# Triangular inversions of four chunks at once in place of two, in a two-layer recurrent decoder on one core

## The chip, the cores and the metric

The kernel runs on one core of one Trainium2 chip. The metric is the device time of one execution in microseconds (us). The core's engines work side by side and meet at semaphores: TensorE (PE; its weight loads are shown as PEld), VectorE (DVE), ScalarE (ACT), GpSimd (POOL) and SyncE (SP), which issues the transfers between HBM and the on-chip memory (SBUF). Matrix products land in PSUM: two tensors here, psA for wide products and psB for small ones, of four banks of 512 columns each.

## The reference

Each of two layers normalizes 512 prompt rows and 8 sample rows of width 1024, projects them, feeds four token mixers, and merges the four results with gates. Two of the mixers, here branch A (RWKV-7) and branch D (gated delta rule), need the inverse of a lower triangular 64 x 64 matrix for each chunk of 64 rows and each of 4 heads. For branch D:

```python
    kb = kc * bc[..., None]
    a_mat = jnp.where(strict, jnp.einsum('nbhid,nbhjd->nbhij', kb, kc) * decay, 0.0)
    m = a_mat + jnp.eye(C, dtype=a_mat.dtype)
    u = lax.linalg.triangular_solve(m, vc * bc[..., None], left_side=True, lower=True)
    w = lax.linalg.triangular_solve(m, kb * jnp.exp(gc)[..., None], left_side=True, lower=True)
...
    def step(S, inp):
        u_i, w_i, qk_i, q_i, k_i, gl_i = inp
        v_new = u_i - jnp.einsum('bhik,bhkv->bhiv', w_i, S)
        o = jnp.einsum('bhik,bhkv->bhiv', q_i, S) + jnp.einsum('bhij,bhjv->bhiv', qk_i, v_new)
        S = S * jnp.exp(gl_i)[..., None, None] + jnp.einsum('bhik,bhiv->bhkv', k_i, v_new)
        return S, o
```

The inversions of different chunks don't depend on each other. The states S run from chunk to chunk, eight chunks in sequence. Branch A's scan is computed in the same chunked form. The 8 sample rows are one decode step each, done on DVE between the chunk work.

## The kernel before

All order is written by hand: each engine has its own program, and named semaphores (`Track`) join them. A layer has four of the phases that matter here in the whole kernel: phase A and phase D of layer 0, then phase A and phase D of layer 1.

**Inversion.** An inversion pass (`j`) treats `GC = 2` chunks, which are 4 pairs of heads (`q`); one phase has `NG = 4` passes. The inverse is built by doubling blocks over `LV = 6` levels. A pass has 11 steps on PE: `pe_start`, then for levels 1 to 5 `pe_y` and `pe_z`. After `pe_y`, ACT copies the product out of PSUM (`act_y`); after `pe_start` and `pe_z`, DVE puts the new blocks in place with two predicated copies (`dve_t`), into T and V, and the next `pe_y` waits for them. The matmuls of `pe_y` and `pe_z` are 32 x 32 tiles, those of `pe_start` and of the chunk work 64 x 64.

**Chunk work.** For each chunk `gram_a` makes the matrices to be inverted and `rows_a` transposes keys and values; then the state runs through `x1_a`, `u_a` and `o_a`. `x1_a(c)` needs the state that DVE wrote after `o_a(c - 1)` (`st_a`), and ACT's copy of that output. These stand behind an inversion step of a later pass. Branch D has the same functions with `_d`.

**Fill.** Behind each step stands `fill_in()`, one slot of wide matmuls (128 x 260, the projection and gate tiles) that need nothing from the chain. A phase has 12 such tiles, each of 12 parts of 4 matmuls, spread evenly over the slots: `SLOTS_A` = 55 slots and `SLOTS_D` = 53. So a slot holds 2 or 3 parts, that is 8 or 12 wide matmuls.

**Transfers.** SP loads the weights of each tile (512 KB) when an earlier tile is done, and in the second half of phase D it also writes out the tanh of each gate tile (260 KB).

## Time and profile before

| what | value |
|---|---|
| median of 3 runs | 1363.7 us (1363.26 to 1364.95) |
| the profiled execution's own time | 1367.13 us |
| its span in the profile | 1365.3 us |
| PE busy | 1318.9 us, 97% of the span |
| DVE busy | 627.7 us, 46% |
| ACT busy | 450.9 us, 33% |
| POOL busy | 375.3 us, 27% |
| mean granted TensorE clock | 0.988 of full speed |

The profile's page gives busy times by engine and groups of instructions; the trace behind it gives each instruction's start. In the rows, "psB<-tg,ws 32*32 32x16 f32 x32" is a group of 32 matmul records that write psB from tg and ws in tiles of 32 x 32, with 16 columns each. One float32 matmul of the program leaves two such records; a wide matmul (psA, 128x260) leaves one. Durations of neighbours on PE overlap, so what a group costs is read from its start to the start of what follows.

### The profile page before, as it was taken

How to read it: one execution, taken by the hardware profiler on the slowest of the kernel's cores; microseconds unless marked ns; L12 is line 12 of the kernel's file. 1: busy time of each engine (PE TensorE's matmuls, PEld its weight loads, DVE VectorE, ACT ScalarE, POOL GpSimd, SP SyncE). 2: the span in 40 equal slices, each digit the busy share in tenths (PEclk: the TensorE clock that was granted, in tenths of full speed). 3: DMA queues.
4: the chain of work that ended last, by engine and by line, in shares of the span. 5: the costliest groups of instructions: out<-in, count | busy, mean ns of one | idle time of the engine just before them, and what ended most of it. 6: DMA issues, size and time to landing. Idle time of an engine off the chain costs nothing.

```text
span 1365.3 us, 40005 instructions
## 1 busy us (share of the span) xinstructions
PE 1318.9 (97%) x18150; PEld 1194.9 (88%) x18150; DVE 627.7 (46%) x1166; ACT 450.9 (33%) x742; POOL 375.3 (27%) x286
## 2 busy tenths in 40 slices
PE   5899999999999999999989999999999999999996
PEld 4899999989899888888779999999988998888896
DVE  4667514318224316756242972242544242467543
ACT  4333422234322236241234253222542222441323
POOL 0344522123222223111323443222332231321122
PEclk9999999999999999999999999999999999999998
DMA  8953231226431263576863333212263223744742
GB/s 314 322 151 84 76 94 49 55 59 131 113 86 49 65 113 105 167 184 194 295 217 89 98 78 87 57 50 65 71 151 105 59 66 62 152 115 104 200 140 94
DMA packets 275933, 162.60 MB, mean 119 GB/s; under 512 B 86102, under 2 KB 244922, under 8 KB 275252
## 3 DMA queue, kind: packets, MB, share of 16 engines
q1 hardware_dynamic: 275220, 159.00, 42.8%
q8 instruction: 143, 2.34, 0.7%
q10 hardware_dynamic: 544, 1.05, 0.2%
q14 instruction: 26, 0.21, 0.1%
HBM read 135.25 MB, written 24.89 MB: 117 GB/s over the span
## 4 chain that ended last, share of the span: by engine, by line
PE 90%; DMA 3%; DVE 3%; ACT 2%; issue 1%; SPq 0%; ACTq 0%; DVEq 0%
PE psA L973 39%; PE psA L981 20%; PE psA L1023 7%; DMA ring<-in_ada_w 2%; PE psB L899 2%; PE psB L915 2%; PE psB L919 1%; PE psB L1126 1%; PE psB L1136 1%; PE psB L320 1%; PE psB L883 1%; PE psB L1364 1%; PE psB L831 1%; PE psB L1089 1%; PE psB L1328 1%
## 5 line engine op out<-in xcount | busy, mean ns | idle before, releaser
L809 POOL TENSOR_TENSOR w_lo<-ring,w_hi 128x512 fp32r<-128x512 f32 x248 | 331.5, 1358 | 835.5 <-ACT w_hi L1668 790.1
L973 PE MATMUL psA<-h_hi,w_hi 128*128 128x260 f32 x1984 | 425.6, 296 | 6.8 <-DVE h_lo L2108 4.9
L973 PE MATMUL psA<-h_lo,w_hi 128*128 128x260 f32 x1984 | 400.9, 284 | 0.0
L973 PEld LDWEIGHTS psA<-h_hi,w_hi 128*128 128x128 f32 x1984 | 305.7, 189 | 28.0 <-issue 15.3
L973 PEld LDWEIGHTS psA<-h_lo,w_hi 128*128 128x128 f32 x1984 | 307.3, 189 | 0.2
L981 PE MATMUL psA<-h_hi,w_lo 128*128 128x260 f32 x1984 | 276.7, 288 | 0.0
L981 PEld LDWEIGHTS psA<-h_hi,w_lo 128*128 128x128 f32 x1984 | 251.7, 189 | 6.9 <-issue 3.0
L1668 ACT CAST w_hi<-ring 128x1024 fp32r<-128x1024 f32 x120 | 123.8, 1032 | 14.6 <-DMA ring<-in_w_in 14.5
L924 ACT COPY ws<-psB 128x128 f32<-128x128 f32 x80 | 21.5, 269 | 187.8 <-PE psB L899 160.0
L1698 ACT ACTIVATE tg<-psA 128x520 f32<-128x520 f32 x48 | 28.9, 603 | 121.0 <-PE psA L981 120.8
L932 DVE COPY_PREDICATED tg<-tmask,psB 128x128 f32<-128x128 uint8 x40 | 14.2, 356 | 101.2 <-PE psB L919 57.6
L932 DVE COPY_PREDICATED ws<-tmask,psB 128x128 f32<-128x128 uint8 x40 | 14.3, 357 | 82.5 <-PE psB L919 44.7
L809 POOL TENSOR_TENSOR rb_lo<-RB,w_hi 128x512 fp32r<-128x512 f32 x16 | 21.6, 1374 | 86.9 <-ACT w_hi L1668 86.9
L809 POOL TENSOR_TENSOR rb_lo<-RB,ra_lo 128x512 fp32r<-128x512 f32 x16 | 21.0, 1339 | 47.5 <-ACT ra_lo L1668 47.5
L1683 ACT COPY RA<-psA 128x520 f32<-128x520 f32 x18 | 10.7, 594 | 62.3 <-PE psA L981 62.2
L2386 DVE SCALAR_TENSOR_TENSOR ws<-RD,parT,ws 128x511 f32<-128x511 f32 (+2 forms) x36 | 30.9, 924 | 0.7 <-ACT ws L1886 0.6
L1023 PE MATMUL psA<-RA,upw 128*128 128x260 f32 x128 | 30.7, 385 | 0.0
L1023 PE MATMUL psA<-RD,upw 128*128 128x260 f32 x128 | 29.9, 384 | 0.8 <-DVE RA L2185 0.8
L1023 PE MATMUL psA<-RB,upw 128*128 128x260 f32 x128 | 29.8, 388 | 0.3 <-DMA upw<-in_w_up 0.2
L2638 DVE SCALAR_TENSOR_TENSOR xT<-psA,modT,xT 128x260 f32<-128x260 f32 x16 | 7.8, 489 | 48.2 <-PE psA L981 36.7
L1023 PE MATMUL psA<-RC,upw 128*128 128x260 f32 x128 | 29.2, 385 | 0.2 <-DMA upw<-in_w_up 0.2
L981 PE MATMUL psA<-merged_hi,rb_lo 128*128 128x260 f32 x224 | 29.1, 282 | 0.0
(511 smaller groups left out, 2000.9 us busy)
## 6 DMA issues: line engine op xcount, KB each, us to landing
ring<-in_w_in SPq DMA_DIRECT2D x122, 512.0 KB, 4.3
scr_tanh<-tg SPq DMA_DIRECT2D x48, 260.0 KB, 4.7
upw<-in_w_up SPq DMA_DIRECT2D x64, 128.0 KB, 3.2
ring<-in_ada_w SPq DMA_DIRECT2D x16, 512.0 KB, 6.4
RB<-in_w_out SPq DMA_DIRECT2D x16, 512.0 KB, 4.2
RA<-scr_tanh SPq DMA_DIRECT2D x30, 260.0 KB, 3.7
ws<-scr_tanh SPq DMA_DIRECT2D x24, 260.0 KB, 3.5
RB<-in_ada_w SPq DMA_DIRECT2D x10, 512.0 KB, 6.2
```

Of the source, the lines that this page charges most:

```text
L320: last = nc.tensor.matmul(out[g:g + 32, 0:256], c32[:, k0 + k, :], piece[:, k, 256 * f:256 * f + 256], start=start, stop=stop)
L809: nc.gpsimd.tensor_tensor(tile_part(RL[s][:, k], (kind, n)), tile_part(RS[s][:, k], (kind, n)), tile_part(HS[L.hslot[q]][:, k], (kind, n)) ...
L899: last = nc.tensor.matmul(meet(z0[pr, cols], lv, 0), At[pr, q, cols], meet(T4[pr, q, cols], lv, 0), start=True, stop=True)
L915: nc.tensor.matmul(meet(z0[pr, cols], lv, 0), V4[pr, q, cols], meet(Y4[pr, q, cols], lv, 0), start=True, stop=True)
L924: nc.scalar.copy(meet(q64(Y), lv, 0), meet(q64(psB[:, 2, 0:256]), lv, 0)).then_inc(*ta.step("y"))
L932: nc.vector.copy_predicated(meet(q64(T), lv, 0), bc(meet(tmask[:, lv, :], lv, 0), 1, 4), meet(q64(psB[:, 2, 0:256]), lv, 0))
L973: nc.tensor.matmul(out(h), HS[L.hslot[q]][:, p, 0:m], cols(part(p), h), start=(p == 0 and part is hi), stop=False)
L981: last = nc.tensor.matmul(out(h), RL[s][:, k, 0:m], cols(hi(k), h), start=False, stop=(k == KT - 1))
L1023: last = nc.tensor.matmul(out(hf), upw[:, idx % UP_RING, i, :], outs[MERGE[idx][0]][:, i, hf * HALF:(hf + 1) * HALF], start=(i == 0), stop ...
L1668: nc.scalar.copy(tile_part(HS[L.hslot[q]], SPLIT[q]), tile_part(RS[s], SPLIT[q])).then_inc(*aw.step("hi"))
L1698: A(half(th_tile(idx)), psA[:, b:b + 2, 0:HALF], ACT.Tanh, scale=0.5).then_inc(*am.step("th"))
L2386: last = STT(out[:, t, sh:SEQ], raw[:, t, 0:SEQ - sh], par(wname, tap * n + t), out[:, t, sh:SEQ], mult, add)
```

## The change

A pass now treats `GQ = 4` chunks, so a phase has two passes (`NQ = 2`) of 11 steps in place of four, and each step has twice the matmuls. The `z` results of the second kind go to psB bank 1 instead of the upper half of bank 2, since bank 2 is now full; the results of `u` and of the state update move from bank 1 to bank 0, and DVE's state update (`st_a`, `st_d`) waits for ACT's copy of the output before it reads bank 0. Of the 24 trips of a phase (`x1`, `u`, `o` of eight chunks) the first 11 stand beside the steps of the second pass and the last 13 behind it, alone with their fill; before, 18 stood beside steps and 6 behind. The slots are recounted: 40 in phase A and 38 in phase D. T has one buffer, which ACT resets at the end of the first pass (`act_t`). V of both passes and the matrices of all chunks are kept at once, so buffers move (some of branch A's to mg5, RB 6 and RB 7). The decode step's pieces on DVE start at the third step of the first pass (before: at the second pass), and their second half stands at the first seven steps of the second pass. The diff, cut:

```diff
-NG = NC // GC
+GQ = 4
+NQ = NC // GQ
...
             def pe_start(pe, tp, At):
-                for q in range(4):
+                for q in range(2 * GQ):
                     for g in range(2):
-                        last = nc.tensor.matmul(psB[sd(g), 2, q * CH:(q + 1) * CH], At[sd(g), q, :], id64[sd(g), :], start=True, stop=True)
+                        last = nc.tensor.matmul(psB[sd(g), 2, q * CH:(q + 1) * CH], At(q)[sd(g)], id64[sd(g), :], start=True, stop=True)
...
-                for q in range(4):
-                    z0, z1 = psB[:, 2, q * CH:(q + 1) * CH], psB[:, 2, 256 + q * CH:256 + (q + 1) * CH]
+                for q in range(2 * GQ):
+                    z0, z1 = psB[:, 2, q * CH:(q + 1) * CH], psB[:, 1, q * CH:(q + 1) * CH]
...
+            def act_t(act, tp, ta, T):
+                act.wait_ge(*tp.at("y", LV - 2))
+                nc.scalar.copy(q64(T), bc(id64, 1, 2 * GQ)).then_inc(*ta.step("ti"))
...
-            SLOTS_A = 5 + 11 * NG + 6
-            SLOTS_D = 3 + 11 * NG + 6
+            STEPS_INV = 2 * LV - 1
+            SLOTS_A = 5 + 2 * STEPS_INV + 13
+            SLOTS_D = 3 + 2 * STEPS_INV + 13
...
+                beside = {0: (gram_a, 4), 1: (gram_a, 5), 2: (rows_a, 0), 3: (rows_a, 1), 4: (gram_a, 6), 5: (rows_a, 2), 6: (gram_a, 7), 7: (rows_a, 3)}
+                late_rows = {7: 4, 9: 5, 10: 6}
+                for j in range(NQ):
+                    At, V = at_a(j), Va[j]
+                    for k in range(STEPS_INV):
...
+                        elif k % 2:
...
+                            pe_y(pe, pa, da, At, Ta, j, (k + 1) // 2)
+                        else:
+                            pe_z(pe, pa, aa, V, Ya, j, k // 2)
+                        if j:
+                            trip_a(k)
+                            if k in late_rows:
+                                rows_a(late_rows[k])
+                        elif k in beside:
+                            work, c = beside[k]
+                            work(c)
+                        fill_in()
+                for n in range(STEPS_INV, 3 * NC):
+                    trip_a(n)
+                    if n == STEPS_INV + 1:
+                        rows_a(7)
                     fill_in()
...
                 def st_a(c):
                     dve.wait_ge(*pa.at("o", c))
-                    did(da, "sum", T_(Ma[:], psB[:, 1, 256:384].rearrange("p (i x) -> p i x", i=2), Ma[:], add), c)
+                    dve.wait_ge(*aa.at("o", c))
+                    did(da, "sum", T_(Ma[:], psB[:, 0, 384:512].rearrange("p (i x) -> p i x", i=2), Ma[:], add), c)
```

What stands in a row on PE. Phase A of layer 0, around the step `pe_y` of level 3 in the first pass, before (line 899 is `pe_y`, lines 915 and 919 `pe_z`, line 1126 `gram_a`, lines 973 and 981 the wide matmuls):

```order
413 L1126 MATMUL psB<-ws 64x128 x8
414 L981 MATMUL psA<-h_hi,w_lo 128x260 x4
415 L973 MATMUL psA<-h_hi,w_hi 128x260 x2
416 L973 MATMUL psA<-h_lo,w_hi 128x260 x2
417 L973 MATMUL psA<-h_hi,w_hi 128x260 x2
418 L973 MATMUL psA<-h_lo,w_hi 128x260 x2
419 L899 MATMUL psB<-tg,ws 32x2x8 x16
420 L973 MATMUL psA<-h_hi,w_hi 128x260 x2
421 L973 MATMUL psA<-h_lo,w_hi 128x260 x2
422 L973 MATMUL psA<-h_hi,w_hi 128x260 x2
423 L973 MATMUL psA<-h_lo,w_hi 128x260 x2
424 L915 MATMUL psB<-ws,tg 32x2x8 x4
```

The same step of the changed kernel (its lines: 906 is `pe_y`, 922 and 926 `pe_z`, 1141 `gram_a`, 1151 `rows_a`, 990 and 998 the wide matmuls):

```order
453 L1141 MATMUL psB<-ws 64x128 x8
454 L998 MATMUL psA<-h_hi,w_lo 128x260 x16
455 L906 MATMUL psB<-tg,mg 32x2x8 x16
456 L906 MATMUL psB<-tg,ws 32x2x8 x16
457 L1151 MATMUL psB<-cst,ws 64x64 x8
458 L1151 MATMUL psB<-cst,RA 64x64 x4
459 L990 MATMUL psA<-h_hi,w_hi 128x260 x2
460 L990 MATMUL psA<-h_lo,w_hi 128x260 x2
461 L990 MATMUL psA<-h_hi,w_hi 128x260 x2
462 L990 MATMUL psA<-h_lo,w_hi 128x260 x2
463 L990 MATMUL psA<-h_hi,w_hi 128x260 x2
464 L990 MATMUL psA<-h_lo,w_hi 128x260 x2
```

One step has 32 matmuls in place of 16, and the wide runs on its two sides have 16 and 12 in place of 12 and 8.

On DVE, at the end of phase A of layer 0, before (lines 932 and 933 are `dve_t`, 2316 `u_a`, 2320 and 2321 `st_a`):

```order
223 L2316 COPY ws<-psB 128x128
224 L2320 TENSOR_TENSOR M<-psB,M 128x128
225 L2321 TENSOR_TENSOR M<-M,pc 128x128
226 L932 COPY_PREDICATED tg<-tmask,psB 128x8x16
227 L933 COPY_PREDICATED tg<-tmask,psB 128x8x16
228 L933 COPY_PREDICATED tg<-tmask,psB 128x4x32
229 L2316 COPY ws<-psB 128x128
230 L2320 TENSOR_TENSOR M<-psB,M 128x128
231 L2321 TENSOR_TENSOR M<-M,pc 128x128
```

The changed kernel at the same end (942 and 948 are `dve_t`, 2247 `u_a`, 2252 and 2253 `st_a`):

```order
196 L948 COPY_PREDICATED RB<-tmask,psB 128x8x32
197 L2247 COPY ws<-psB 128x128
198 L2252 TENSOR_TENSOR M<-psB,M 128x128
199 L2253 TENSOR_TENSOR M<-M,pc 128x128
200 L2247 COPY ws<-psB 128x128
201 L2252 TENSOR_TENSOR M<-psB,M 128x128
202 L2253 TENSOR_TENSOR M<-M,pc 128x128
203 L2247 COPY ws<-psB 128x128
204 L2252 TENSOR_TENSOR M<-psB,M 128x128
205 L2253 TENSOR_TENSOR M<-M,pc 128x128
```

The predicated copies are over four chunks earlier, and the states of the last five chunks follow each other with nothing between but their own waits.

## Rows read from the trace of the kernel before

**Rows 1.** The page: busy time, share and instructions of each engine.

```profile
PE 1318.9 (97%) x18150; PEld 1194.9 (88%) x18150; DVE 627.7 (46%) x1166; ACT 450.9 (33%) x742; POOL 375.3 (27%) x286
```

**Rows 2.** Windows, the four phases: length, busy by engine, granted clock, DMA share, GB/s.

```profile
166.70:300.88 134.18, 134.18 (x3137) 122.13 (x3137) 38.09 (x102) 33.97 (x77) 31.17 (x24) 1.00 0.24 62
383.54:508.60 125.06, 123.05 (x2813) 111.83 (x2813) 37.50 (x99) 30.27 (x69) 29.41 (x23) 0.99 0.34 78
832.61:966.97 134.36, 134.36 (x3137) 122.24 (x3137) 38.06 (x102) 34.07 (x77) 31.17 (x24) 1.00 0.24 62
1049.00:1175.13 126.13, 124.23 (x2820) 112.59 (x2819) 37.48 (x99) 30.27 (x69) 30.06 (x24) 0.99 0.35 79
```

**Rows 3.** Timeline of PE, phase A, layer 0: y, wide, z, wide, y.

```profile
180.08 0.44 PE L899 MATMUL psB<-tg,ws 32*32 32x16 f32 x32
180.45 0.50 PE L973 MATMUL psA<-h_hi,w_hi 128*128 128x260 f32 x2
...
182.08 0.25 PE L915 MATMUL psB<-ws,tg 32*32 32x16 f32 x8
...
182.74 0.50 PE L973 MATMUL psA<-h_hi,w_hi 128*128 128x260 f32 x2
...
183.89 0.44 PE L899 MATMUL psB<-tg,ws 32*32 32x16 f32 x32
184.26 1.70 PE L981 MATMUL psA<-h_hi,w_lo 128*128 128x260 f32 x12
```

**Rows 4.** Timeline of PE: the last z step of a pass.

```profile
200.53 0.44 PE L910 MATMUL psB<-tg,ws 32*32 32x32 f32 x16
200.90 0.39 PE L973 MATMUL psA<-h_hi,w_hi 128*128 128x260 f32 x1
```

**Rows 5.** Timeline of PE: 16 and 32 records of 64 x 64 before a wide run.

```profile
261.41 0.68 PE L883 MATMUL psB<-cst,ws 64*64 64x64 f32 x16
262.02 0.39 PE L973 MATMUL psA<-h_hi,w_hi 128*128 128x260 f32 x1
...
407.04 1.15 PE L1364 MATMUL psB<-cst,ws 64*64 64x64 f32 x32
408.12 0.51 PE L973 MATMUL psA<-h_hi,w_hi 128*128 128x260 f32 x2
```

**Rows 6.** Timeline of DVE: the two copies of `dve_t` at level 1.

```profile
182.87 0.45 DVE L932 COPY_PREDICATED tg<-tmask,psB 128x128 f32<-128x128 uint8 x1 [3.07 <-PE psB L919]
183.12 0.50 DVE L933 COPY_PREDICATED tg<-tmask,psB 128x128 f32<-128x128 uint8 x1
```

**Rows 7.** Timelines of PE, ACT and DVE between `o_a` and the next `x1_a`.

```profile
292.62 0.50 PE L973 MATMUL psA<-h_hi,w_hi 128*128 128x260 f32 x2
...
294.25 0.33 PE L1152 MATMUL psB<-M,ws 64*64 64x64 f32 x4
...
292.74 0.27 ACT L1832 COPY RA<-psB 128x128 f32<-128x128 f32 x1 [0.26 <-PE psB L1183]
...
292.74 0.29 DVE L2320 TENSOR_TENSOR M<-psB,M 128x128 f32<-128x128 f32 x1 [2.65 <-PE psB L1183]
293.07 0.92 DVE L2321 TENSOR_TENSOR M<-M,pc 128x128 f32<-128x128 f32 x1
```

**Rows 8.** The page's row of PE's instruction queue: packets, MB, share.

```profile
q8 instruction: 143, 2.34, 0.7%
```

**Rows 9.** A stop of PE in phase D, and windows behind it and over one block.

```profile
484.98 0.24 PE L919 MATMUL psB<-ws 32*32 32x16 f32 x6 [1.27 <-issue]
...
485.50:490.50 5.00, 5.00 (x78) 4.63 (x75) 0.75 (x4) 0.80 (x3) 0.00 (x0) 0.66 0.54 59
...
1141.00:1145.50 4.50, 4.50 (x71) 4.12 (x71) 0.47 (x2) 0.80 (x3) 0.00 (x0) 0.62 0.01 4
...
398.75:399.00 0.25, 0.25 (x27) 0.22 (x30) 0.00 (x0) 0.00 (x0) 0.00 (x0) 1.00 0.23 66
```

**Rows 10.** Timeline of SP: the last of the vector transfers for branch D's decode step.

```profile
391.73 0.43 SPq L590 DMA_DIRECT2D vv<-scr_b  x1
```

More of the change, by code:

```diff
@@ L893, in pe_y @@
                             first, second = quarter(g, 0), quarter(g, 1)
-                            last = nc.tensor.matmul(z0[second, lower], At[first, q, upper], T4[first, q, lower], start=True, stop=True)
+                            last = nc.tensor.matmul(z0[second, lower], At(q)[first, upper], T4[first, q, lower], start=True, stop=True)
                         continue
@@ L1244, in _, with trip_a @@
-                for c in (NC - 2, NC - 1):
-                    x1_a(c)
-                    fill_in()
-                    u_a(c)
-                    fill_in()
-                    o_a(c)
+                def trip_a(n):
+                    (x1_a, u_a, o_a)[n % 3](n // 3)
+                for c in range(GQ):
+                    gram_a(c)
+                    fill_in()
+                fill_in()
+                beside = {0: (gram_a, 4), 1: (gram_a, 5), 2: (rows_a, 0), 3: (rows_a, 1), 4: (gram_a, 6), 5: (rows_a, 2), 6: (gram_a, 7), 7: (rows_a, 3)}
@@ L1462, in _ @@
+                for n in range(STEPS_INV, 3 * NC):
+                    trip_d(n)
+                    if n == STEPS_INV + 1:
+                        rows_d(3)
                     fill_in()
@@ L1875, in _, with trip_a @@
-                for c in (NC - 2, NC - 1):
-                    x1_a(c)
-                    after_fill()
-                    after_fill()
-                    o_a(c)
+                tree_start(Ta, Va, aa)
+                for c in range(GQ + 1):
+                    after_fill()
+                rows_at = {2: 0, 3: 1, 5: 2, 7: 3}
+                late_rows = {7: 4, 9: 5, 10: 6}
+                def trip_a(n):
+                    if n % 3 != 1:
+                        (x1_a, None, o_a)[n % 3](n // 3)
@@ new lines, in _ @@
+                for j in range(NQ):
+                    for k in range(STEPS_INV):
+                        if k % 2:
+                            act_y(act, pa, aa, Ya, j, (k + 1) // 2)
+                        if j == 0 and k == STEPS_INV - 2:
+                            act_t(act, pa, aa, Ta)
+                        if j:
+                            trip_a(k)
+                        here = (late_rows if j else rows_at)
+                        if k in here:
+                            rows_a(here[k])
+                        after_fill()
@@ L1880, in _ @@
+                for n in range(STEPS_INV, 3 * NC):
+                    trip_a(n)
+                    if n == STEPS_INV + 1:
+                        rows_a(7)
                     after_fill()
@@ L2365, in _ @@
+                for n in range(STEPS_INV, 3 * NC):
+                    trip_a(n)
                 pd, ad, dd = TR["pe_d"], TR["act_d"], TR["dve_d"]
@@ new lines, in _, with trip_d @@
+                gram_d(1)
+                def trip_d(n):
+                    if n % 3 != 1:
+                        (x1_d, None, st_d)[n % 3](n // 3)
+                beside = {0: (gram_d, 2), 2: (gram_d, 3), 4: (rows_d, 0), 6: (rows_d, 1)}
+                for j in range(NQ):
+                    dve.wait_ge(*ad.at("ti", j))
+                    for k in range(STEPS_INV):
+                        if k % 2 == 0:
+                            dve_t(dve, pd, dd, GRd, 2, Td, Vd[j], j, k // 2)
+                        if j:
+                            trip_d(k)
+                            if k == 7:
+                                rows_d(2)
+                        elif k in beside:
+                            work, c = beside[k]
+                            work(c)
+                        if j == 0 and 2 <= k < 9 or j and k < 7:
+                            decode_d(k if j else k - 2, j)
@@ L2535, in _ @@
+                for n in range(STEPS_INV, 3 * NC):
+                    trip_d(n)
+                    if n == STEPS_INV + 1:
+                        rows_d(3)
                 ac, dc = TR["act_c"], TR["dve_c"]
-                for c in (NC - 2, NC - 1):
-                    x1_d(c)
-                    st_d(c)
                 dve.wait_ge(*ac.at("cv0"))
```

452 lines of the change are left out of this document (135 added, 317 removed).

## The prediction

> **What bounds the kernel now.** I read the page's busy times first: PE is busy for 1318.9 of 1365.3 us and DVE for less than half of that [rows 1]. So only what shortens PE's own row of work, or a wait on it, can move the time. Then I cut out the four phases that the change touches, by windows. The two phases A last 134.18 and 134.36 us, and PE is busy in every microsecond of them: no semaphore costs anything there, neither of DVE's copies nor of ACT's. The two phases D last some 125.6 us each, and PE stands still for 2.01 and 1.90 us in them [rows 2]. The reader is to see that the latency of the inversion is already hidden by the fill. A change that only hides it better has nothing to win in phase A.
>
> So the question is what a step costs PE beyond its matmuls. I read that from starts in the timeline. A run of 12 wide matmuls takes from 180.45 to 182.08, 1.63 us; a run of 8 from 182.74 to 183.89, 1.15 us [rows 3]. Four matmuls make the difference of 0.48, so one costs 0.12, and a run of 8 would be 0.96 without its 0.19. That 0.19 us is lost once per run, whenever PE comes from small tiles to wide ones and goes back. In the same way a y step with 32 records takes 180.45 - 180.08 = 0.37 us and a z step with 64 takes 182.74 - 182.08 = 0.66 us [rows 3]: 0.29 for 32 records, and 0.08 once per step. The last z step, 16 records in tiles with twice the columns and half as many side by side, takes 0.37 as well [rows 4], as if it were 32. For 64 x 64 tiles, 16 records take 0.61 us and 32 take 1.08 [rows 5]: 0.47 for 16 records, and 0.14 once.
>
> As a test of this reading I sum phase A from it. Wide: 576 x 0.12 + 54 runs x 0.19 = 79.4. The 20 y steps are 7.4 and the 20 z steps 16 x 0.66 + 4 x 0.37 = 12.0. The rest (starts, grams, rows, chunk trips) are the other 35 us of the 134.2 [rows 2], and the change leaves their number as it is, save the starts.
>
> **The change, part by part.**
>
> *Matmuls.* Two passes with eight q stand for four with four: no matmul is added or removed. The fill is the same 144 parts.
>
> *Fewer runs.* The slots go from 55 to 40 in phase A and from 53 to 38 in phase D; in each kernel two of them are neighbours, so the wide runs go from 54 to 39 and from 52 to 37. 15 runs x 0.19 = 2.85 us per phase.
>
> *Fewer steps.* 40 y and z steps become 20, each with twice the records: 20 x 0.08 = 1.6 us per phase (y then takes 0.66, z 0.66 + 64 x 0.009 = 1.24). Four starts become two: 2 x 0.14 = 0.28.
>
> *Chunk work.* Its instructions are the same; more of it stands alone between wide runs, but these runs are counted above. Nothing is taken for it.
>
> The sum is 4.73 us per phase, x 4 = 18.9 us.
>
> *Longer copies on DVE.* The two copies of a low level take 0.45 and 0.50 us, the second 0.25 behind the first, and end 0.88 us after the z step (182.74 to 183.62) [rows 6]. With twice the elements I bound each at twice its duration, so the pair ends at most 0.13 + 0.50 + 1.00 = 1.63 us after the step. The cover is a fill of 12 or 16 wide matmuls, 1.63 us or 2.11, and at the low levels chunk work of 8 to 40 records ahead of it. If that chunk work were gone, the low levels would just be even. I take zero; the upper bound is 0.2 x 2 steps x 8 passes = 3.2 us.
>
> *The added wait.* Between `o_a` and the next `x1_a` DVE now waits for ACT's copy. Before, `o_a` ends at 292.62; ACT copies for 0.27 from 292.74 and at the same time DVE starts a sum and a product that end at 293.99, and the next `x1_a` starts at 294.25, behind 12 wide matmuls [rows 7]. With ACT first, everything on DVE comes some 0.4 us later: 294.4, that is 0.15 late behind 12 wide matmuls and in time behind 16. The 0.92 of the product is its long form. Beside a step of the inversion 0.66 us or more is added to the cover; behind the second pass there are four such places in a phase. Queued behind DVE's wait is only the next `u` copy, and PE is the one that waits for that. 4 x 4 x 0.15 = 2.4 us is the bound if every one is the long form with the short fill; I take 0.8, a third. The bound below is nothing.
>
> *Inputs that are wanted earlier.* Branch D's decode begins two steps into the first pass. The last vector transfer is issued at 391.73 [rows 10]. In the new order two grams, three slots, and three steps with two grams stand between 383.5 and that piece, about 2.0 + 5.1 + 8.7 us, so it is wanted near 399; 7 us are enough. Zero.
>
> *PE's instructions.* PE's instruction queue moves 2.34 MB in 143 packets [rows 8]: 16.4 KB each. With one load and one matmul for each of 18150 records [rows 1] this is 64 bytes an instruction and 127 records a block. In quiet time such a block shows as a lone quarter microsecond at 66 GB/s [rows 9]. In phase D PE stops in the middle of a z step, with nothing to wait for, for 1.27 us up to 484.98 [rows 9]. There are six such stops, three in each phase D, which make up the 2.0 and 1.9 us of [rows 2]. After the longest in each, the granted clock is 0.66 for 5 us and 0.62 for 4.5 us [rows 9], 1.7 us lost each time. I read them as instruction blocks that come late behind SP's tile loads; together they cost 3.9 + 3.4 = 7.3 us. They stand in the half of phase D in which tanh tiles are written out too. After the change most of that half is behind the second pass, where a slot has only 8 to 40 small records, so blocks are wanted seldom; this speaks for a gain of up to 7.3. But inside the passes a z step is 128 records, a whole block in 1.24 us, where before the densest stretch (z, 12 wide, y: 108 records) took 0.66 + 1.63 + 0.37 = 2.66 us. This speaks for new stops, in phases A too. I take zero between the two.
>
> The Trainium skill ("Runtime: NRT & Kernel Launch", Instruction fetch mechanics) says that PE's instruction memory holds 128 KiB, filled in blocks of 16 KiB. The block size agrees with [rows 8]; eight blocks ahead would be over 30 us of work and no stop could come, in either kernel. The same section also speaks of only two lines, which fits the stops in [rows 9] better. By the deep memory the sum stays as it is, since the stops would have another cause.
>
> **The sum.** The profiled execution took 1367.1 us: 1367.1 - 18.9 + 0.8 = 1349.0. The median is 3.4 us below the profiled execution, so 1363.7 - 18.1 = **1345.6 us**.
>
> **The rivals.**
>
> *Late instruction blocks eat the gain.* For it: six stops already, and records up to 2.5 times as dense inside the passes (9.7 ns each for 24.6). Against it: phases A have the same loads and not one stop. One late block with its slow stretch is 1.3 + 1.7 = 3.0 us. Three more than now give 1354.6, and that is the likely form. It decides from seven more on: 21 us, 1366.6, slower than before. Each phase has 22 of its 40 or 38 slots inside the passes and so about seven of its 12 tile loads, 28 in all, so seven are possible.
>
> *Late blocks go away.* The stops of phase D vanish because the tanh tiles fall behind the second pass: 1345.6 - 7.3 = 1338.3.
>
> *Waits take the place of the hidden ones.* All bounds of the longer copies and of the added wait at once: 3.2 + 2.4 - 0.8 = 4.8 more; and as much again, 4.8, if ACT is still busy with a tile's evacuation when `o_a` ends. 1345.6 + 9.6 = 1355.
>
> *The change doesn't do what it says.* If the 0.19 and 0.08 were not paid per run and per step but overlapped with something that stays, the kernel would end at 1363 to 1364. Against it: the same two numbers rebuild the 134.2 us of phase A.
>
> **How the numbers follow.** The forecast, 1340 to 1351: 0.70. Some late blocks, 1351 to 1361: 0.11; many, over 1366: 0.04. Blocks that go away, 1336 to 1340: 0.07. Waits, 1351 to 1358: 0.05. Nothing saved: 0.03. The range 1337 to 1355 holds the forecast and most of its two neighbours, 0.83. 0.2% is 2.7 us, about what a measurement of this kernel tells from no change: faster 0.93, same 0.03, slower 0.04.
>
> **What the next profile would show.** Right: phases A near 129.5 us with PE busy throughout; y steps of 0.66 and full z steps of 1.24; wide runs of 12 and 16 at 1.63 and 2.11. The added wait: idle time before `x1_a` or `x1_d` behind the second pass. The blocks: stops "issue" inside z steps, with a granted clock near 0.6 behind them. I am wrong if a step with twice the records takes twice as long, if PE idles in phase A, or if the stops in the two phases D together change by more than 4 us.

## The result, and the profile after

The changed kernel is slower: 1376.5 us median of 11 runs (1368.57 to 1382.66) against 1363.8 of 11 runs of the kernel before (1359.48 to 1366.14) on the same chip. The ratio is 1.0083, with a 95% interval of 1.0057 to 1.0108. The forecast was 1345.6. The profiled execution of the changed kernel took 1382.66 us, the slowest of the 11 and 6 more than their median, so its profile shows more of the harm than a usual execution has. The kernel's executions scatter by 6 to 8 us to either side of their median, those of before by 2 to 4.

The page gives PE's busy time and its instruction queue. They answer to [rows 1] and [rows 8]:

```profile
PE 1313.4 (95%) x18150; PEld 1197.9 (87%) x18150; DVE 620.4 (45%) x1086; ACT 442.9 (32%) x686; POOL 373.9 (27%) x286
q8 instruction: 143, 2.34, 0.7%
```

PE has the same 18150 records, its instruction queue moves the same 143 packets (called blocks from here on), and PE is busy for 5.5 us less, but the span is 15.5 us longer. So PE stands still for some 21 us more than before. The windows of the four phases answer to [rows 2] (length, busy by engine, granted clock, DMA share, GB/s):

```profile
168.16:305.76 137.60, 132.01 (x3138) 122.33 (x3138) 37.40 (x82) 32.15 (x63) 31.74 (x24) 0.98 0.23 60
386.92:514.23 127.31, 120.91 (x2818) 111.94 (x2817) 33.41 (x79) 28.26 (x55) 28.82 (x23) 0.97 0.32 75
838.61:977.16 138.55, 132.58 (x3137) 122.84 (x3137) 37.52 (x82) 32.16 (x63) 31.73 (x24) 0.98 0.23 60
1061.34:1189.33 127.99, 121.80 (x2818) 112.87 (x2818) 34.25 (x79) 28.46 (x55) 28.34 (x23) 0.96 0.32 75
```

The four lengths add up to 531.5 us, against 519.7 in [rows 2]. Length less busy time gives the idle time: 5.59, 6.40, 5.97 and 6.19, together 24.2 us, where [rows 2] has 3.9. And the clock, which was full in phases A, is below 1.00 in every phase. What PE waited for is in its list of waits (line waited at, releaser, us in total, times, longest):

```profile
PE psB L906 <- issue: 8.3, 5, 2.6
...
PE psB L926 <- issue: 8.0, 8, 1.6
...
PE psB L922 <- issue: 3.4, 4, 1.7
...
PE psB L1191 <- issue: 1.5, 1, 1.5
PE psB L1195 <- issue: 1.3, 1, 1.3
...
PE psB L901 <- issue: 0.5, 1, 0.5
```

That is 20 stops of 23.0 us in which PE waited for nothing that the profile shows, 18 of them inside the y and z steps (lines 901, 906, 922, 926). Before, the same list has five stops of 3.8 us, all in phases D. A stretch of the timeline of PE, phase A of layer 0, shows one of them, and what comes behind it:

```profile
185.20 0.44 PE L906 MATMUL psB<-tg,mg 32*32 32x16 f32 x32
185.48 0.45 PE L906 MATMUL psB<-tg,ws 32*32 32x16 f32 x32
185.86 1.09 PE L1141 MATMUL psB<-ws 64*64 64x128 f32 x16
186.88 1.71 PE L998 MATMUL psA<-h_hi,w_lo 128*128 128x260 f32 x12
...
188.99 0.25 PE L922 MATMUL psB<-RB,tg 32*32 32x16 f32 x8
...
190.18 0.68 PE L1151 MATMUL psB<-cst,ws 64*64 64x64 f32 x16
...
192.67 0.36 PE L906 MATMUL psB<-tg,mg 32*32 32x16 f32 x20
195.55 0.34 PE L906 MATMUL psB<-tg,mg 32*32 32x16 f32 x11 [2.52 <-issue]
...
196.31 1.12 PE L1151 MATMUL psB<-cst,ws 64*64 64x64 f32 x16
```

Up to 192.67 all is about as forecast: y takes 0.66 us (185.20 to 185.86), z 1.19 (188.99 to 190.18; the forecast was 1.24), 16 wide matmuls 2.11 (186.88 to 188.99). Then PE stops after 20 of the 64 records of a y step and goes on 2.52 us later. What follows is slow: the same 16 records of L1151 that took 0.52 us at 190.18 take 0.90 at 196.31. Two windows, behind this stop and over one y-to-y pair, show why:

```profile
195.55:201.50 5.95, 5.95 (x84) 5.60 (x83) 0.00 (x0) 0.85 (x2) 0.00 (x0) 0.50 0.01 3
...
185.20:192.67 7.47, 7.47 (x262) 6.90 (x261) 3.08 (x6) 2.40 (x4) 2.43 (x2) 1.00 0.34 96
```

Behind the stop the granted clock is 0.50 for six microseconds, the 1.2 GHz level of the two. The last row is the rate at which a pass wants instructions: 262 records in 7.47 us, or 128 in 3.65 us. The window over the same kind of stretch in the kernel before, y, wide, z, wide of [rows 3]:

```profile
180.08:183.89 3.81, 3.81 (x117) 3.48 (x117) 0.75 (x2) 0.95 (x2) 2.53 (x2) 1.00 0.62 190
```

That is 128 records in 4.17 us, and PE never stops in it.

How a block arrives is seen in a stretch of the changed kernel in which no other transfer runs: windows over the end of a z step and the stop behind it, and the timeline of PE where it goes on.

```profile
232.25:232.50 0.25, 0.25 (x32) 0.22 (x22) 0.00 (x0) 0.00 (x0) 0.25 (x1) 1.00 0.00 0
232.50:232.75 0.25, 0.25 (x11) 0.25 (x12) 0.13 (x1) 0.00 (x0) 0.25 (x1) 1.00 0.22 66
232.75:234.90 2.15, 0.89 (x31) 0.81 (x26) 1.17 (x2) 0.00 (x0) 0.06 (x1) 1.00 0.00 0
...
236.00:236.25 0.25, 0.25 (x4) 0.25 (x3) 0.22 (x2) 0.00 (x0) 0.00 (x0) 1.00 0.22 66
```

```profile
234.97 0.27 PE L1195 MATMUL psB<-ws 64*64 64x64 f32 x2 [1.33 <-issue]
```

The block begins to move between 232.50 and 232.75, and PE goes on at 234.97, some 2.3 us later, with no other transfer in between. A window counts a transfer's bytes and time where it begins, so the block did not move in a quarter microsecond, as [rows 9] were read: 0.22 of 16 engines for 0.25 us is 0.88 us of one engine, and 0.7% of 16 engines' span for 143 blocks is some 1.1 us each. The next block begins to move at 236.00, 1.0 us after PE went on. I read this as a cycle: 1.0 us from entering a block until the next begins to move, 0.9 for the transfer, 1.4 until its first matmul, together some 3.4 us for 128 records.

The long stop at 195.55 is of another kind. SP had issued a tile load and a tanh write when PE entered a block at about 189.5 (128 records before the stop), and the next block began to move only when they were through:

```profile
188.62 0.38 SPq L634 DMA_DIRECT2D ring<-in_w_in  x1
189.25 0.37 SPq L659 DMA_DIRECT2D scr_tanh<-mg  x1
...
189.50:193.25 3.75, 3.53 (x146) 3.20 (x135) 2.90 (x5) 1.14 (x2) 3.01 (x2) 1.00 0.73 211
193.25:193.50 0.25, 0.00 (x0) 0.00 (x0) 0.25 (x1) 0.00 (x0) 0.04 (x1) 1.00 0.25 66
193.50:195.50 2.00, 0.00 (x0) 0.00 (x0) 0.33 (x1) 0.00 (x0) 0.00 (x0) 0.87 0.00 0
```

From entering to the start of the transfer are 3.8 us in place of 1.0; from there to PE's restart are 2.3, as in the quiet stop. The 128 records took 3.56 us, so with a transfer after 1.0 us this stop would hardly have been there. I read the packets of the instruction queue at all 20 stops in the same way, counting back 128 records to where PE entered the block ahead (127 where it had gone on from another stop there), which is good to some tenths of a microsecond. Each ends 2.3 to 2.8 us after its block begins to move. At nine of them, 15.3 of the 23.0 us, other transfers of 460 to 790 KB stood between entering and the block, which began to move 1.7 to 3.8 us after entering. At the other eleven, 7.7 us, nothing over 5 KB did, and it was 0.8 to 1.8 us. In the kernel before, all five stops are of the loaded kind (1.8 to 4.1 us). This is the one of [rows 9]:

```profile
478.20 0.37 SPq L632 DMA_DIRECT2D ring<-in_w_in  x1
478.84 0.36 SPq L657 DMA_DIRECT2D scr_tanh<-tg  x1
...
478.50:482.50 4.00, 3.92 (x99) 3.56 (x88) 0.79 (x3) 1.52 (x3) 2.52 (x2) 1.00 0.77 196
482.50:482.75 0.25, 0.25 (x5) 0.25 (x4) 0.00 (x0) 0.00 (x0) 0.00 (x0) 1.00 0.54 119
```

**Where the time went.** In the profiled executions the phases became 11.7 us longer, in two parts. Idle time grew by 24.2 - 3.9 = 20.3. Busy time fell only by 8.5 (507.3 after, 515.8 in [rows 2]), because part of it ran at half clock. Read in windows of 0.25 us, the clock is down in six stretches (four of 3.4 us, one of 6.8 and one of 10.2) and costs 15.4 us, against two stretches of 3.4 and 3.4 us lost before: 12.0 more. So the work itself shrank by 8.5 + 12.0 = 20.5 us, where the prediction has 18.9. 20.3 + 12.0 - 20.5 = 11.8, and some 3.8 more fell outside the four phases, where nothing was changed.

### The profile page after: what moved, and what is told of

It reads as the page before. It is cut to its first block, busy times and chain, and to the rows that moved or that the text cites. A ratio compares the mean times of both kernels' runs of the same rounds, so it can differ in the third digit from the quotient of the medians.

```text
span 1380.8 us, 39829 instructions
## 1 busy us (share of the span) xinstructions
PE 1313.4 (95%) x18150; PEld 1197.9 (87%) x18150; DVE 620.4 (45%) x1086; ACT 442.9 (32%) x686; POOL 373.9 (27%) x286
## 3 DMA queue, kind: packets, MB, share of 16 engines
q8 instruction: 143, 2.34, 0.7%
## 4 chain that ended last, share of the span: by engine, by line
PE 87%; DMA 4%; issue 2%; DVE 2%; ACT 2%; SPq 2%; ACTq 0%; DVEq 0%
PE psA L990 38%; PE psA L998 19%; PE psA L1040 7%; DMA ring<-in_ada_w 2%; PE psB L906 2%; PE psB L922 2%; PE psB L926 1%; PE psB L1141 1%; PE psB L322 1%; PE psB L1151 1%; DMA RB<-in_ada_w 1%; SPq L407 1%; ACT w_hi L1632 1%; PE psB L890 1%; DMA upw<-in_w_up 1%
## 5 line engine op out<-in xcount | busy, mean ns | idle before, releaser
L990 PE MATMUL psA<-h_lo,w_hi 128*128 128x260 f32 x1984 | 406.4, 287 | 0.0
L990 PEld LDWEIGHTS psA<-h_hi,w_hi 128*128 128x128 f32 x1984 | 312.0, 192 | 25.8 <-issue 15.3
L990 PEld LDWEIGHTS psA<-h_lo,w_hi 128*128 128x128 f32 x1984 | 313.2, 192 | 0.2
L998 PE MATMUL psA<-h_hi,w_lo 128*128 128x260 f32 x1984 | 272.5, 287 | 0.0
L942 DVE COPY_PREDICATED tg<-tmask,psB 128x256 f32<-128x256 uint8 x20 | 11.1, 553 | 79.0 <-PE psB L926 46.3
L942 DVE COPY_PREDICATED ws<-tmask,psB 128x256 f32<-128x256 uint8 x20 | 11.0, 552 | 75.3 <-PE psB L926 60.7
L931 ACT COPY ws<-psB 128x256 f32<-128x256 f32 x20 | 7.5, 376 | 79.5 <-PE psB L906 60.5
L2411 DVE SCALAR_TENSOR_TENSOR M<-M,kdl,psB 128x64 f32<-128x64 f32 x32 | 7.6, 278 | 56.7 <-ACT RD L1874 56.7
L2301 DVE SCALAR_TENSOR_TENSOR ws<-RD,parT,ws 128x511 f32<-128x511 f32 (+2 forms) x36 | 30.9, 925 | 0.7 <-ACT ws L1832 0.6
```

Source lines behind the costliest of these rows:

```text
L942: nc.vector.copy_predicated(meet(q64(T), lv, 0), bc(meet(tmask[:, lv, :], lv, 0), 1, 2 * GQ), meet(q64(psB[:, 2, :]), lv, 0))
L990: nc.tensor.matmul(out(h), HS[L.hslot[q]][:, p, 0:m], cols(part(p), h), start=(p == 0 and part is hi), stop=False)
L998: last = nc.tensor.matmul(out(h), RL[s][:, k, 0:m], cols(hi(k), h), start=False, stop=(k == KT - 1))
L2301: last = STT(out[:, t, sh:SEQ], raw[:, t, 0:SEQ - sh], par(wname, tap * n + t), out[:, t, sh:SEQ], mult, add)
```

## The experiments

Theory T (S in the texts that were written ahead of the runs): a block of some 127 instruction records can only be had every so often. Inside the longer passes PE uses them up faster than that, and behind some of the stops the clock is down too. Rival L: blocks are late because SP's tile loads are ahead of them, as the prediction read it. The two don't exclude each other: a load can lengthen the time that a block takes, and the density decides whether PE notices. Rival B: the moved results (psB bank 0) and DVE's added wait do the damage. All ratios are to the kernel before, run on the same chip in the same job.

**burst: the supply by itself.** The kernel before, with 512 additional matmuls (1024 records) that nothing reads, behind phase A of layer 0, where the DMA engines are nearly idle:

```diff
                 last.then_inc(*pa.step("mt"))
+                if layer == 0:
+                    for n in range(512):
+                        g, e = n % 2, n // 2 % 2
+                        pr = quarter(g, e)
+                        nc.tensor.matmul(psB[pr, 2, 16 * (n // 4 % 16):16 * (n // 4 % 16) + 16], id64[pr, lower], id64[pr, 0:16], start=True, stop=True)
```

> The kernel before, with 512 extra small matmuls (1024 records, 8 instruction blocks of 127 records; 32 x 32 tiles, 16 columns, four tiles in turn, constant operands, results never read) on TensorE behind phase A of layer 0, where no tile load runs. It measures how fast instructions can be supplied. Theory S (supply: in the changed kernel's stops a block becomes usable about 3.6 us after the one ahead of it is entered, load or no load): after one or two blocks the burst goes at one block in 3.6 us, so it lasts 22 to 29 us and shows stops of 2 to 2.5 us that end 2.4 us behind each lone block transfer. Theory L (blocks only come late behind tile loads): nothing delays them here, 1024 x 0.009 = 9.5 us without a stop.

1393.7 us in one run, 30 more than the kernel before. The timeline of PE over the additional records, and a window over all of them:

```profile
300.94 1.34 PE L1260 MATMUL psB<-cst 32*32 32x16 f32 x139
303.86 1.25 PE L1260 MATMUL psB<-cst 32*32 32x16 f32 x128 [1.57 <-issue]
307.58 1.90 PE L1260 MATMUL psB<-cst 32*32 32x16 f32 x128 [2.48 <-issue]
311.04 1.90 PE L1260 MATMUL psB<-cst 32*32 32x16 f32 x128 [1.56 <-issue]
...
321.95 1.90 PE L1260 MATMUL psB<-cst 32*32 32x16 f32 x128 [1.83 <-issue]
325.40 1.78 PE L1260 MATMUL psB<-cst 32*32 32x16 f32 x117 [1.55 <-issue]
```

```profile
300.94:327.12 26.18, 13.81 (x1026) 13.04 (x1025) 0.00 (x0) 5.37 (x9) 2.49 (x2) 0.58 0.10 24
```

This is the row to remember: PE runs exactly 128 records, stops, and runs the next 128. From one restart to the next it takes 3.45 to 3.73 us, whether the 128 records take 1.25 us (full clock) or 1.90 (half). By the queue's packets that is 1.0 to 1.1 us until the next block begins to move, 0.9 to 1.3 for the transfer and 1.3 to 1.5 until its first matmul. The additional 1024 records take 26.2 us instead of some 10. The changed passes want 128 records in 3.65 us, which is inside that range. The first stop comes after 139 records, so no more was in hand than the rest of one block and one more.

Of this the Trainium skill ("Runtime: NRT & Kernel Launch", Instruction fetch mechanics) says that blocks are of 16 KiB and that crossing into a new one is mostly hidden. The block's size agrees with this case (143 blocks are 2.34 MB). That it is hidden holds for most crossings of the kernel before, and for none of the seven here from the 139th record on.

**bank0: the moved results alone.** The kernel before, with u and the state's sum in psB bank 0 and the added wait, nothing else:

```diff
                     dve.wait_ge(*pa.at("o", c))
-                    did(da, "sum", T_(Ma[:], psB[:, 1, 256:384].rearrange("p (i x) -> p i x", i=2), Ma[:], add), c)
+                    dve.wait_ge(*aa.at("o", c))
+                    did(da, "sum", T_(Ma[:], psB[:, 0, 384:512].rearrange("p (i x) -> p i x", i=2), Ma[:], add), c)
```

> The kernel before with one part of the change alone: the results of u and of the state update lie in psB bank 0, and the state update on VectorE waits for ScalarE's copy of the output. Passes of two chunks as before. Theory S: within 2 us of the kernel before, 1362 to 1367, because the density of matmul records is as it was; at most some short waits before x1. Rival B (the shared bank or the added wait causes the stops of TensorE): 1370 or more, with stops in phases A.

1365.6 us, ratio 1.0013 (0.9993 to 1.0034). The profile has six small stops (0.2 to 0.7 us), five in phases D, at the lines of those of before, and one of 0.2 in a phase A. B falls: it could explain 5 us at most, not 31.

**light: the changed kernel with easier tile loads.** The loads of the tiles of the phases read their 512 KB as one contiguous piece per partition from another weight, so these tiles are computed from wrong weights.

```diff
+                    if (kind, n) in IN_A + IN_D:
+                        sp.dma_start(RS[s].rearrange("p k c -> p (k c)"), a["w_out"][layer, 0:P, :]).then_inc(arrived, 16)
+                        return
                     sp.dma_start(RS[s], src.rearrange("(k p) c -> p k c", p=P)).then_inc(arrived, 16)
```

> The changed kernel with the tile loads made lighter inside phases A and D: each of the 24 tiles of a layer that fill these phases is loaded as 128 rows of 4 KB from another weight (so the projections of these tiles are computed from the wrong weights), where before it was 1024 rows of 512 bytes. Same bytes, in an eighth of the descriptors, so each load keeps the queues busy for a shorter time. Theory S: most stops stay, since they come with the queues quiet as well: 1370 to 1380. Theory L: the stops go with the load, and the kernel falls to 1345 to 1355.

1367.3 us, ratio 1.002 (0.9997 to 1.0043): some 9 us less than the changed kernel, a little below what T expected and far above what L alone did. The profile has 17 stops of 15.0 us, where the changed kernel has 20 of 23.0; but this profile is of the fastest of ten executions (1361.8 us) and that one of the slowest of 11, so the difference of the two flatters the edit. One stop in the same place as the one at 195.55:

```profile
193.26 0.27 PE L909 MATMUL psB<-tg,mg 32*32 32x16 f32 x11 [1.56 <-issue]
```

It took 1.56 us in place of 2.52 (its twin in layer 1: 1.59 in place of 2.60), and the clock behind it stayed at 1.00. The nine loaded stops of the changed kernel are all there again and all but one shorter, 9.1 us in place of 15.3: their blocks began to move 1.4 to 2.9 us after entering, in place of 1.7 to 3.8. The quiet ones make up 5.9 us, where the changed kernel has 7.7. So loads make a block later, and where they do they lengthen the stop. The loads still moved as many bytes, so this is not a test without load; the quiet stop at 234.97 and burst are.

**coarse: fewer records, more work.** The changed kernel with the y and z steps of levels 1 to 4 in 64 x 64 tiles, half as many records in these steps, each longer:

```diff
-                    for e, cols in enumerate((lower, upper)):
-                        for g in range(2):
-                            pr = quarter(g, e)
-                            last = nc.tensor.matmul(meet(z0[pr, cols], lv, 0), At(q)[pr, cols], meet(T4[pr, q, cols], lv, 0), start=True, stop=True)
+                    for g in range(2):
+                        pr = sd(g)
+                        last = nc.tensor.matmul(meet(z0[pr], lv, 0), At(q)[pr], meet(T4[pr, q], lv, 0), start=True, stop=True)
```

> The changed kernel with the y and z steps of levels 1 to 4 in tiles of 64 x 64 in place of 32 x 32: half the instructions for the same products (the blocks off the diagonal that this adds are masked away by the copies). Two tiles side by side in place of four, so a y step should take 0.9 to 1.1 us for 0.66 and a z step 1.8 to 2.0 for 1.2, which adds 20 to 39 us over four phases. Semaphores, passes, banks and fill stay as in the changed kernel. Theory S: the records in a pair of slots fall from about 250 to 150, and the stops inside the steps vanish: TensorE idle under 1 us in each phase A, where the changed kernel has 5.6. Rival B (banks, waits or the length of the passes cause the stops): the idle time stays near 5 us a phase.

1371.7 us in one run. Its list of waits has no "issue" at all, its clock is full in all four windows (those of layer 0):

```profile
167.66:304.30 136.64, 136.19 (x2370) 127.44 (x2369) 38.10 (x82) 32.33 (x63) 30.87 (x24) 1.00 0.23 60
388.47:512.92 124.45, 124.45 (x2049) 116.68 (x2049) 33.25 (x79) 28.25 (x55) 28.78 (x23) 1.00 0.32 76
```

A y step takes 0.95 us with 32 records, a z step about 1.9 with 64, so PE does 0.29 and 0.7 us more per step, 8 x 0.99 = 7.9 per phase, 31.7 in all. The prediction's own sum then closes: 1363.6 - 18.9 - 7.3 (no stops, no slow clock) + 0.8 + 31.7 = 1369.9. This was decisive for the density: the same passes, the same banks, the same loads, a quarter fewer records in a phase (2370 for 3138), and every stop is gone, the loaded ones too. The sum also agrees with the saving of 18.9 us, within the scatter of a single run.

**weighted: denser fill inside the passes.** The changed kernel with 4 or 5 parts of fill behind each step of a pass and 2 or 4 in the tail, in place of 3 or 4 everywhere:

```diff
-            fill_a, fill_d = Fill(IN_A, SLOTS_A), Fill(IN_D, SLOTS_D)
+            fill_a, fill_d = Fill(IN_A, [2] * 5 + [5 - k % 2 for k in range(STEPS_INV)] * 2 + [4 if n % 3 == 2 and n < 23 else 2 for n in range(STEPS_INV, 24)]), Fill(IN_D, [3, 3, 4] + [5 - k % 2 for k in range(STEPS_INV)] * 2 + [4 if n % 3 == 2 and n < 23 else 2 for n in range(STEPS_INV, 24)])
```

> The changed kernel with only the fill weighted (4 and 5 parts a slot inside the passes, 2 behind most of the work around them); all tiles 32 x 32 as in the changed kernel. Theory S: a full z step is still a block in 1.2 us, less than the 3.6 a block needs, but the long runs behind it let the supply catch up, so the stops get fewer or shorter, not rare: 1358 to 1372. Rival: if the mean density inside the passes alone decided (252 records in 7.9 us, 4.0 us a block), no stop would be left: 1338 to 1350.

1361.1 us, ratio 0.999 (0.9972 to 1.0007), 15 us less than the changed kernel with the same matmuls in another order. Two windows, phases A and D of layer 0:

```profile
167.12:299.23 132.11, 129.56 (x3137) 119.82 (x3137) 40.26 (x82) 32.38 (x63) 30.35 (x24) 1.00 0.24 63
383.29:510.38 127.09, 120.75 (x2818) 111.85 (x2818) 37.37 (x79) 28.51 (x55) 28.40 (x23) 0.97 0.34 77
```

In phase A PE is busy for 129.56 us, the forecast's 129.5, at full clock; the y-to-y pair has 269 records in 8.41 us, 128 in 4.00. Phase D still loses 6.3 us to idle time and some to the clock. The profile has 16 stops of 12.8 us in all, though the mean density is below what burst could be supplied with: a z step is still a block's worth of records in 1.2 us, and at eleven of the 16 stops a load of over 300 KB stood ahead of the block.

**zsplit: half of the slot inside the z step.** As weighted, with half of the slot's fill between the two halves of a z step:

```diff
                 for q in range(2 * GQ):
+                    if q == GQ and lv < LV - 1:
+                        between()
```

> The weighted kernel with each z step of levels 1 to 4 cut in two halves of 64 records and half of the slot's fill between them. This adds 16 wide runs and 16 step beginnings a phase, 16 x 0.27 x 4 = 17 us if all were paid at once (8 z steps a phase are cut: 8 x 0.27 x 4 = 8.6 us). Theory S: 127 records from the start of a z step take about 2.5 us in place of 1.2 to 1.9, so the stops are shorter than in the weighted kernel: 1352 to 1366.

1362.5 us, ratio 0.9993 (0.9978 to 1.0009): no better than weighted. The profile has six stops of 5.7 us in place of 16 of 12.8, so the size of one burst does matter, beside the average over a pair. What was won on the stops was paid back in the steps: the additional change from small tiles to wide ones and back is 0.19 + 0.08 = 0.27 us by the prediction's prices, 2.2 us for the eight split steps of a phase; the phase A of layer 1 is busy for 131.7 us in place of 129.4.

**mix and mix_even: half of each z step coarse.** z of the first four q in 64 x 64 tiles, on weighted's fill (mix) and on the changed kernel's own even fill (mix_even):

```diff
+                    if q < GQ:
+                        for g in range(2):
+                            pr = sd(g)
+                            nc.tensor.matmul(meet(z0[pr], lv, 0), V4[pr, q], meet(Y4[pr, q], lv, 0), start=True, stop=True)
+                        for g in range(2):
+                            pr = sd(g)
+                            nc.tensor.matmul(meet(z1[pr], lv, 1), Y4[pr, q], meet(V4[pr, q], lv, 1), start=True, stop=True)
+                        continue
```

> A version meant to keep the gain without the stops. The changed kernel, with the z steps of levels 1 to 4 for the first four q in 64 x 64 tiles and for the other four in 32 x 32 (96 records in place of 128), and the fill weighted: 4 parts behind each y step and 5 behind each start and z step, 2 behind most of the work ahead of and behind the passes. Theory S: a z step takes about 1.55 us (half of 1.9 and half of 1.2), 0.35 more, 11 us in all; in no stretch do 127 records take much less than 3.6 us, so few stops are left. 1363.6 - 18.9 - 7.3 (the stops of the kernel before) + 11.2 + 0.8 = 1349.4 without a stop, 1349 to 1358 with some. Rival L (stops come with the tile loads, whatever the density): 1370 or more.

> The same half-coarse z steps in the changed kernel with its even fill (3 or 4 parts a slot). It tells what the weighting of the fill is worth. Theory S: 127 records from the start of a z step then take about 3.9 us in quiet time, so stops come only where a tile load delays a block: 1352 to 1362, a few us above the weighted one.

mix took 1359.5 us, ratio 0.9975 (0.9957 to 0.9992); mix_even 1363.9, ratio 1.0009 (0.9993 to 1.0026). They are 1.5 and 1.9 us above the ranges that T expected. Issue stops fell to 1.4 us in mix; in mix_even 4.7 us remained, all in phases A, while its phases D had none and were the shortest (120.66 and 120.39 us).

**both: each phase with what suited it.** Weighted fill and fine tiles in phases A; the even fill and half-coarse z steps in phases D.

```diff
-                            pe_z(pe, pd, ad, V, Yd, j, k // 2)
+                            pe_z(pe, pd, ad, V, Yd, j, k // 2, GQ)
```

> The best parts of the runs so far, by phase. Phase A as in the weighted kernel (32 x 32 tiles, 4 and 5 parts of fill a slot inside the passes), phase D as in the kernel with half-coarse z steps and even fill. In their profiles the phases A of the one lasted 132.1 and 131.8 us, the phases D of the other 120.7 and 120.4; the kernel before has 134.2, 125.6, 134.4 and 125.5. Theory S, if the phases add up: 14.7 us less than before, 1348 to 1352. If the place of the block boundaries in the program moves the stops about (each changed phase shifts all blocks behind it), part of that is lost: up to 1358.

1357.6 us, ratio 0.996 (0.9943 to 0.9977), faster than both kernels; from mix, which ran on another chip, the intervals don't tell it apart. It is 4.9 us less than before, where the sum of the phases had promised 14.7. Its windows:

```profile
169.23:301.93 132.70, 129.63 (x3137) 119.89 (x3136) 40.21 (x82) 32.34 (x63) 30.33 (x24) 1.00 0.24 63
384.49:505.85 121.36, 120.49 (x2561) 112.07 (x2561) 33.41 (x79) 28.26 (x55) 28.79 (x23) 1.00 0.33 78
829.11:962.91 133.80, 131.29 (x3138) 121.41 (x3137) 40.24 (x82) 32.34 (x63) 30.34 (x24) 0.99 0.24 62
1045.46:1165.87 120.41, 120.38 (x2561) 112.02 (x2561) 33.50 (x79) 28.36 (x55) 28.80 (x23) 1.00 0.34 79
```

The four add up to 508.3 us, 11.4 less than [rows 2]; 6.5 are still idle time. Its profile has six stops of 4.6 us, five of them in phases A. Why the medians show less than the phases isn't settled; the profiled execution of before was 3.4 us above its median, which is half of that gap.

**before_light: the light loads in the kernel before.** The edit of light, made in the kernel before (so these tiles are computed from wrong weights too).

> The kernel before with the lighter tile loads inside phases A and D (128 rows of 4 KB from another weight for 1024 rows of 512 bytes, so these tiles are computed from the wrong weights). Theory: its six stops need both a tile load that delays a block and a dense stretch. With the lighter loads the stops in phase D should shrink or go: 1356 to 1361. If they had another cause, the time stays within 2 us of the kernel before.

1361.9 us, ratio 0.9994 (0.998 to 1.0009). Its profile has stops of only 2.3 us, the longest 1.0, and no slow clock in phases D, where the kernel before has 3.9 and 3.4 us. Its median doesn't show these 5 us and is what the other branch expected (within 2 us of before). All four of its stops have a load ahead of their block, lighter as it is. What other executions of the kernel before lose to stops, one profile doesn't tell; this stays unclear.

**thin: the kernel before, with less fill inside its passes.** The old passes of two chunks, 2 parts behind every step, the rest ahead of and behind them:

```diff
+            fill_a, fill_d = Fill(IN_A, [5] * 5 + [2] * (11 * NG) + [5, 5, 5, 5, 5, 6]), Fill(IN_D, [7, 6, 6] + [2] * (11 * NG) + [6, 6, 6, 6, 6, 7])
```

> The kernel before, passes of two chunks, with the fill moved out of the passes: 2 parts in each of their 44 slots (before: 2 or 3) and the rest ahead of and behind them. Number of matmuls, steps and wide runs stay. Theory S (the density of the records makes the stops, not the passes of four chunks): z, 8 wide, y and x1 are 127 records in about 3.1 us, less than 3.6, so stops of up to 0.5 us appear in phases A, which had none; 2 to 8 us in all phases together more than before: 1366 to 1375, besides waits for VectorE or ScalarE, which the profile names as such. Rival (only the change's passes bring stops): phase A stays without a stop that has no releaser.

1366.5 us in one run. Here T expected more stops than came: 1.4 us in the profile's list, none over 0.5, and no slow clock in phase A or D of layer 0. (One more wait of 1.2 us, put down to a copy of ACT at line 924 that was done 0.8 us earlier, ends 2.4 us after a block began to move, as the stops do.) One window shows the density:

```profile
198.76:202.92 4.16, 4.16 (x137) 3.77 (x137) 0.49 (x2) 0.75 (x2) 1.95 (x2) 1.00 0.26 76
```

137 records in 4.16 us are 128 in 3.89. That is denser than before (4.17) but still slower than the supply (3.45 to 3.73). Phase A of layer 0 had stops here that it had not before (0.3, 0.4 and 0.2 us), so density alone brings some, but little. The mean density can't be the whole reason: weighted lost 12.8 us at 128 in 4.00. Its z steps of 128 records, where thin has 64, are what differs by design; that this is the cause isn't shown beyond zsplit.

## Why the prediction was wrong

- **Matmuls, Fewer runs, Fewer steps** (18.9 us): right. The steps took 0.66 and 1.19 us (forecast 0.66 and 1.24), the wide run of 16 took 2.11 as forecast. Phase A, where its blocks keep up, is busy for 129.56 us (forecast 129.5). In the changed kernel itself the saving measures 20.5 us.
- **Longer copies on DVE** (0, bound 3.2): right. No wait of PE in the four phases is put down to DVE's predicated copies.
- **The added wait** (0.8): right, with luck in the exact number, since 0.8 was a third of a bound. PE's waits there are two of 0.8 us in sum for DVE (L1167, `x1_a`). A third of 0.2 (L1383, `o_d`) is for ACT's copy of `u`, which PE waited for in the kernel before as well. The tail of phase A on ACT and DVE shows the order that was foreseen, the sum behind the copy:

```profile
270.56 0.27 ACT L1797 COPY RA<-psB 128x128 f32<-128x128 f32 x1 [0.26 <-PE psB L1197]
...
270.92 0.29 DVE L2252 TENSOR_TENSOR M<-psB,M 128x128 f32<-128x128 f32 x1 [4.19 <-ACT RA L1797]
271.25 0.56 DVE L2253 TENSOR_TENSOR M<-M,pc 128x128 f32<-128x128 f32 x1
```

- **Inputs that are wanted earlier** (0): right, no such wait.
- **PE's instructions** (taken at zero): this is the step that failed. Measured against the kernel before it is 20.3 us of idle time, 1.0 of it the two waits above, and 12.0 of half clock: 31 us in the profiled execution. Between the medians it is 1376.5 - 1345.6 = 30.9; that the two agree is partly luck, since the profile is of the slowest execution.

Why it failed can be named. The prediction read the stops of [rows 9] rightly as instruction blocks that come late behind SP's transfers: all five (it counted six, three in each phase D; the list has two and three) have 410 to 800 KB ahead of their block. What it lacked is that a block takes its time with no load at all, 3.45 to 3.73 us in burst. It supposed that a stop needs a load ahead of its block; eleven of the 20 stops in the changed kernel had none. And it took "phases A have the same loads and not one stop" as a sign that their loads were harmless. They were so only at the old density. With 128 records in 4.17 us at the densest, phases A went through their loads without a stop; at 3.65 the same kind of load costs 2.52 and 2.60 us there. The change went to 3.65 for the very reason for which it was to win: fewer slots of fill inside the passes. Zero "between the two" had no sum behind it.

The demand was set against the wrong measure too. "Up to 2.5 times as dense" compares one z step of the changed kernel (9.7 ns a record) with z, 12 wide and y of the kernel before (24.6). A z step of before takes 0.66 us for 64 records, which is about as dense (10.3 ns); over a pair of steps the rise is from 4.17 to 3.65 us, a seventh.

The rival **Late instruction blocks eat the gain** is what happened; it was said to decide "from seven more on", and there were 15 more. Its price of 3.0 us per stop with its slow clock was somewhat high (31 us for 15 are 2.1 each). Its chance of 0.04 was the mistake.

What the rows of before could have told: the records of a y-to-y pair over its length, next to the places where a load makes a block late. [rows 2] has the other hint: stops come in phases D alone.

What stays open. How the idle time divides between density and loads was read from one execution, the slowest; about two thirds of it stood behind loads there. Where blocks begin relative to the steps moves with every edit ahead of them, so single stops come and go, and I did not vary this by itself. What decides which stop is followed by a slow clock is open (see the last section). Why the stops of phases D in the kernel before got shorter in the profile of before_light but its median did not fall is not settled.

## What to carry to other kernels

Count the instructions of TensorE per microsecond in the densest stretch, not only its busy time. In this kernel small float32 matmuls were supplied at about 128 records (64 matmuls) in 3.5 to 3.7 us, and at 4.2 to 6.1 us where a load of half a megabyte had been issued just ahead; a stretch longer than a block that wants them faster stops, and after some of the stops runs at half clock for a while. Wide matmuls between small ones are not only cover for latency, they also give the supply its time; put them where the small ones are dense, or take larger tiles for part of them, even at more busy time. When a stop with no releaser stands in a trace, ask two things before blaming either: what the supply can do by itself (a thousand idle matmuls are enough), and when the block's transfer began after the block ahead of it was entered.

## What the hardware showed that I had not expected

- Blocks of 128 records came no faster than every 3.45 to 3.73 us with DMA nearly idle (burst): 1.0 to 1.1 us until the next block began to move, 0.9 to 1.3 for the transfer, 1.3 to 1.5 until its first matmul.
- A tile load and a tanh write issued just ahead made the block begin to move 3.8 us after entering in place of 1.0 (stop at 195.55). The same stop is there twice, 2.52 and 2.60 us, and with the lighter loads 1.56 and 1.59.
- The length of a stop doesn't tell whether the clock falls. Of the changed kernel's twelve stops of over 1 us in the phases, six had a slow stretch beginning at them or within 1.3 us (the one of 2.52: clock 0.50 for 6.8 us, from before PE went on); behind those of 1.33, 1.34, 1.27, 1.25, 1.59 and 1.60 it stayed at 1.00. In the kernel before a stop of 1.04 was followed by one. A stretch of 3.4 us costs 1.7.
- Stops keep the clock down: over burst's 26.2 us the granted clock is 0.58, and it is still 0.50 in the 5.3 us behind it. 26.2 us and the 2.6 that these slow wide matmuls lose make up nearly all of the 30 that the run cost.
